# Output mixers of a two-block network: inputs and weight splits taken into the latent attention, first two tiles interleaved

## What is computed

```
for l in range(2):
    h = rms_norm(x, norm_w[l]) * (1 + scale) + shift
    proj = h @ w_in[l]                           # split by columns
    r_o = rms_norm(retention(rope(rq), rope(rk), rv))
    m_o = mla(mq, mkv, mkr, ...)                 # latent attention, 8 heads
    g_o = rms_norm(gla(gq, gk, gv, gg, w_g2[l], b_g2[l]), gla_norm[l])
    mixed = concat(r_o * silu(rz), m_o * silu(mz), g_o * silu(gz))
    x = x + gate * (mixed @ w_out[l])
return rms_norm(x, final_norm)
```

## Time and profile before

| | us |
|---|---|
| median of 3 runs (4027.2 to 4030.54) | 4028.1 |
| the profiled execution, its own time | 4022.91 |
| its span, first to last instruction | 4021.1 |
| of it: second latent attention (3581.0 to 3804.9) | 223.9 |
| start of the second mixer, to its first projection product (3804.9 to 3867.3) | 62.4 |
| start of the first mixer (3057.4 to 3119.6) | 62.2 |

### The profile page before, as it was taken

The page is one execution under the profiler, slowest core; times in us unless marked ns, Lnnn a source line. Parts: engine busy times, 40 slices in busy tenths (PEclk is TensorE's granted clock), DMA queues, the critical chain, the costliest instruction groups (busy, mean ns, idle before and its releaser), DMA issues. The chain is left out here.

```text
span 4021.1 us, 52306 instructions
## 1 busy us (share of the span) xinstructions
PE 3400.3 (85%) x17620; PEld 2687.7 (67%) x17620; DVE 2374.9 (59%) x3722; ACT 1875.8 (47%) x3128; POOL 308.8 (8%) x374
## 2 busy tenths in 40 slices
PE   8988979599999448786999992699895979989778
PEld 7876658488888324575888882578674757877656
DVE  3226666799988637548999885551234645313276
ACT  3115641378888310115788882331345623224474
POOL 0000001000000110000000002000001300000032
PEclk9999989699999769887999996899997989999879
DMA  6322234499999665436999996442223234322232
GB/s 236 106 69 62 64 99 165 161 399 398 399 398 398 240 242 184 160 129 229 399 398 399 399 398 216 168 157 81 61 49 119 98 134 157 115 59 49 74 130 78
DMA packets 411311, 791.67 MB, mean 197 GB/s; under 512 B 99942, under 2 KB 154758, under 8 KB 408968
## 3 DMA queue, kind: packets, MB, share of 16 engines
q1 hardware_dynamic: 388108, 705.61, 48.6%
q0 software_dynamic: 13824, 50.34, 3.6%
q10 hardware_dynamic: 9216, 33.56, 2.1%
HBM read 653.45 MB, written 135.95 MB: 196 GB/s over the span
## 5 line engine op out<-in xcount | busy, mean ns | idle before, releaser
L312 DVE TENSOR_TENSOR experts_down_lo<-weights_down,experts_down_hi 128x1024 fp32r<-128x1024 f32 x256 | 301.1, 1222 | 56.5 <-ACT experts_down_hi L308 54.2
L312 DVE TENSOR_TENSOR experts_gate_lo<-weights_gate,experts_gate_hi 128x1024 fp32r<-128x1024 f32 x256 | 298.8, 1222 | 52.1 <-ACT experts_gate_hi L308 51.4
L308 ACT CAST experts_gate_hi<-weights_gate 128x1024 fp32r<-128x1024 f32 x256 | 254.2, 1056 | 106.5 <-PEq L126 67.8
L312 DVE TENSOR_TENSOR experts_up_lo<-weights_up,experts_up_hi 128x1024 fp32r<-128x1024 f32 x256 | 296.3, 1221 | 1.2 <-ACT experts_up_hi L308 0.5
L359 PE MATMUL project_acc<-project_wh,project_hh 128*128 128x512 f32 (+2 forms) x768 | 286.1, 373 | 0.0
L360 PE MATMUL project_acc<-project_wl,project_hh 128*128 128x512 f32 (+2 forms) x768 | 282.3, 368 | 0.0
L361 PE MATMUL project_acc<-project_wh,project_hl 128*128 128x512 f32 (+2 forms) x768 | 282.3, 368 | 0.0
L308 ACT CAST experts_down_hi<-weights_down 128x1024 fp32r<-128x1024 f32 x256 | 255.8, 1052 | 24.9 <-DMA weights_down<-in_moe_w_down_dram 24.7
L308 ACT CAST experts_up_hi<-weights_up 128x1024 fp32r<-128x1024 f32 x256 | 253.9, 1056 | 7.8 <-DMA weights_up<-in_moe_w_up_dram 6.2
L2248 ACT COPY project_row<-project_acc 128x512 f32<-128x512 f32 (+2 forms) x96 | 51.8, 540 | 380.0 <-PE project_acc L361 380.0
L359 PE MATMUL experts_yp<-experts_down_hi,experts_hTh 128*128 128x512 f32 x512 | 210.6, 411 | 13.1 <-DVE experts_hTl L312 13.1
(11 more groups left out here) (427 smaller groups left out, 8045.8 us busy)
## 6 DMA issues: line engine op xcount, KB each, us to landing
weights_gate<-in_moe_w_gate_dram SPq DMA_DIRECT2D x256, 512.0 KB, 12.9
weights_up<-in_moe_w_up_dram SPq DMA_DIRECT2D x256, 512.0 KB, 12.2
weights_down<-in_moe_w_down_dram SPq DMA_DIRECT2D x256, 512.0 KB, 11.4
scratch_y<-experts_y ACTq DMA_DIRECT2D x64, 512.0 KB, 6.3
pool_ada<-in_ada_w_dram SPq DMA_DIRECT2D x16, 1536.0 KB, 7.7
project_raw<-in_w_in_dram SPq DMA_DIRECT2D x8, 2048.0 KB, 9.8
scratch_proj<-project_row SPq DMA_DIRECT2D x64, 256.0 KB, 2.0
qkv_raw<-in_attn_w_qkv_dram SPq DMA_DIRECT2D x48, 256.0 KB, 3.4
```

What stands on the lines that cost most here:

```text
L308: return act.copy(hi, src)
L312: return dve.tensor_tensor(lo, src, hi.bitcast(F32), ALU.subtract)
```

## The change

A new holder, `MixAhead`, spans the attention and the mixer of a layer. It owns `w` (now with 2 stages of raw rows), `g2`, `bg`, `gn`, `row` and `vv`, and their semaphores; it is a `Phase` of its own, with its own exit. The attention gets it as `prefetch`. SyncE issues, behind the loads of the first two heads, two rows of the weights, the three small vectors, and row tiles and values 0 and 1; later heads load weight rows 2 to 7. In the third pair of each head ScalarE and VectorE split one row.

The mixer starts without these. SyncE loads the attention's output rows, the output gate (with a semaphore of its own, first waited for ahead of the first residual), the final gain and the residual. The chains of tiles 0 and 1 are written interleaved; tile 1 puts its gate products into the bank of `acc[0]` (`small_bank`), `elast` has two places, and `gla_scores` waits for the parts of the tile before. From i = 1 the loops are the ones of before.

```
@@ phase_attention @@
                 load_q(1)
                 load_v(1)
+                if prefetch:
+                    prefetch.load_first(nc, sp)
...
                         load_q(h + 2)
+                    if prefetch and h + 2 < KC:
+                        prefetch.w.load(sp, h + 2)
...
                         for mp in range(maps):
                             exp(n + 1, 1, mp)
+                    if prefetch and i == 2:
+                        prefetch.w.split_hi(act, n // PAIRS)
...
                     if what == "q" and h < HEADS:
                         copy_q(part, h)
+                    if prefetch and n % PAIRS == 2:
+                        prefetch.w.split_lo(dve, n // PAIRS)
@@ new class MixAhead(Phase) @@
+        self.w = SplitRows(self, self.w_out, stages=2)
...
+    def load_first(self, nc, sp):
+        for k in range(2):
+            self.w.load(sp, k)
+        sp.dma_start(self.g2[:, :], self.w_g2).then_inc(self.small_in, 16)
...
+        sp.dma_start(self.gn[:, :], self.gla_norm.partition_broadcast(P)).then_inc(self.small_in, 16)
+        for i in range(2):
+            self.load_row(sp, i)
+            self.load_vv(sp, i)
@@ phase_mix_out @@
-    SMALL = 80 if final else 64
+    SMALL = 48
...
+        def small_bank(i):
+
+            return acc[0][:, :].rearrange("p (a b) -> p a b", a=4) if i == 1 else sc
...
                 pe.wait_ge(q_past, i + 1)
-                Tr(sc[:, 2, :], kwT[:, :], K["ident"]).then_inc(kwt_ready, 1)
+                if i > 0:
+                    pe.wait_ge(ag_ready, i)
+                Tr(small_bank(i)[:, 2, :], kwT[:, :], K["ident"]).then_inc(kwt_ready, 1)
...
                 open_tile(1)
+                gate_and_retention(1)
                 gla_scores(0)
                 updates(0)
-                gate_and_retention(1)
-                for i in range(T):
+                gla_scores(1)
+                outputs(0)
+                open_tile(2)
+                updates(1)
+                gate_and_retention(2)
+                mixed_transposes(0)
+                for i in range(1, T):
@@ ScalarE @@
                 copies(0)
                 softplus(0)
-                w.split_hi(act, 0)
+                copies(1)
                 exponents(0)
...
+                softplus(1)
+                exponents(1)
                 silus(0)
                 silus(1)
...
+                take_outputs(0)
+                copies(2)
+                silus(2)
@@ VectorE @@
                 gate_sums(0)
-                w.split_lo(dve, 0)
+                gate_in(1)
+                retention_scores(1)
                 gla_operands(0)
-                w.split_lo(dve, 1)
+                gate_sums(1)
                 gla_parts(0)
-                w.split_lo(dve, 2)
                 states(0)
-                for i in range(T + 2):
+                gla_operands(1)
+                gla_parts(1)
+                mean_squares(0)
+                gated(0)
+                states(1)
+                normalized(0)
+                for i in range(1, T + 2):
@@ body @@
+                with MixAhead(nc, f"ahead{l}", proj, A["gla_w_g2_2"][l], A["gla_b_g2_2"][r, :], A["gla_norm_2"][r, :],
+                              A["w_out_2"][l]) as ahead:
+                    mla_attention(nc, K, f"mla{l}", mq, mk, mkv, mla_o, totals, ahead)
```

More of the change, by code:

```diff
@@ L2363, in _, with mla_attention @@
                         finish_mla(j)
-def mla_attention(nc, K, name, mq, mk, mkv, out, totals):
+def mla_attention(nc, K, name, mq, mk, mkv, out, totals, ahead):
     def tiles(ap, base, step, width):
@@ L2370, in mla_attention, with __init__, __enter__, load_row @@
     phase_attention(nc, K, name, tiles(mq, 0, MQ, MQ), tiles(mk, 0, MQ, MQ), tiles(mkv, NOPE, NOPE + MV, MV),
-                    tiles(out, 0, MV, MV), 1, MQ, MV, K["chunked"], MQ ** -0.5, totals)
-def phase_mix_out(nc, K, name, proj, mla_o, x, w_g2, b_g2, gla_norm, w_out, mod, final_norm, out):
+                    tiles(out, 0, MV, MV), 1, MQ, MV, K["chunked"], MQ ** -0.5, totals, prefetch=ahead)
+class MixAhead(Phase):
+    SEGS = (("rq", "rk"), ("rz", "rz"), ("mz", "gk"), ("gg", "gz"))
+    ROW = sum(COLS[b][1] - COLS[a][0] for a, b in SEGS)
+    def __init__(self, nc, name, proj, w_g2, b_g2, gla_norm, w_out):
+        super().__init__(nc, name)
+        self.proj, self.w_g2, self.b_g2, self.gla_norm, self.w_out = proj, w_g2, b_g2, gla_norm, w_out
+    def __enter__(self):
+        super().__enter__()
+        self.w = SplitRows(self, self.w_out, stages=2)
+        self.g2, self.bg, self.gn = self.sb("g2", [GRANK, P]), self.sb("bg", [P, 1]), self.sb("gn", [P, GDV])
+        self.row = self.sb("row", [P, 2, self.ROW])
+        self.vv = self.sb("vv", [P, 2, 2, 256])
+        self.small_in = self.sem("small_in")
+        self.row_in, self.vv_in = ([self.sem(f"{n}{b}") for b in range(2)] for n in ("row_in", "vv_in"))
+        return self
+    def load_row(self, sp, i):
+        at = 0
+        for a, b in self.SEGS:
+            c0, c1 = COLS[a][0], COLS[b][1]
+            sp.dma_start(self.row[:, i % 2, at:at + c1 - c0], self.proj[i * P:(i + 1) * P, c0:c1]).then_inc(self.row_in[i % 2], 16)
+            at += c1 - c0
+    def load_vv(self, sp, i):
+        for n, c in enumerate(("rv", "gv")):
+            sp.dma_start(self.vv[:, i % 2, n, :], self.proj[i * P:(i + 1) * P, COLS[c][0]:COLS[c][1]]).then_inc(self.vv_in[i % 2], 16)
+    def load_first(self, nc, sp):
+        for k in range(2):
+            self.w.load(sp, k)
+        sp.dma_start(self.g2[:, :], self.w_g2).then_inc(self.small_in, 16)
+        with nc.allow_non_contiguous_dma(reason="one bias per partition"):
+            sp.dma_start(self.bg[:, :], self.b_g2.rearrange("o (p a) -> p (o a)", a=1)).then_inc(self.small_in, 16)
+        sp.dma_start(self.gn[:, :], self.gla_norm.partition_broadcast(P)).then_inc(self.small_in, 16)
+        for i in range(2):
+            self.load_row(sp, i)
+            self.load_vv(sp, i)
@@ L2382, in phase_mix_out @@
+def phase_mix_out(nc, K, name, ahead, mla_o, x, mod, final_norm, out):
     T = TILES
     final = final_norm is not None
-    SEGS = (("rq", "rk"), ("rz", "rz"), ("mz", "gk"), ("gg", "gz"))
+    SEGS = ahead.SEGS
     at, col_at = 0, {}
@@ L2788, in _ @@
                         softplus(i + 1)
-                    if i == 0:
-                        for k in range(6, KC):
-                            w.split_hi(act, k)
                     if has(i):
@@ L2940, in _ @@
                         final_scale(i - 2)
-                    if i == 0:
-                        for k in range(4, 6):
-                            w.split_lo(dve, k)
                     if has(i):
```

117 lines of the change are left out of this document (43 added, 74 removed).

## The result

The changed kernel takes 4046.1 us (median of 20 runs, 4009.0 to 4075.6) against 4027.9 of the kernel before (20 runs, 4020.5 to 4033.4): ratio 1.0047, 95% interval 1.0032 to 1.0062. It is **slower by 18 us**, where 10 us less was forecast, and outside the range given; the slowest of the twenty, over 1.5% above the fastest, is left out of the ratio. The scatter is a result too: 67 us between its runs, 13 us before. The clock granted to TensorE, averaged over an execution, goes with it: 0.925 in the run of 4009.0 us, 0.915 in the profiled one, 0.909 in the one of 4075.6.

What follows compares the result with a forecast made beforehand. TensorE was taken to bound the attention and steady mixer, with time to win in the two starts. Starts -40.8, stalls +25.6, clock +4, exit +1 gave -10.2 us: 4017.9 from 4028.1, range 3994 to 4036.

Steps and rivals of the forecast that it cites:

- The starts: Stage start to first projection product in each mixer: falls from 62.4 to 42.0 us, -20.4 per mixer, -40.8 for two.
- operands of tile 1 to the end of its scores: 3.5 us: Step in the mixer's start, after tile 0's states at 22.0: takes 3.5 us, done at 25.5.
- the bound of 46: Slow bound of the mixer's start: about 46 us (-16) if GpSimd's scaling slows VectorE's operands and tile 1's scores come late.
- The stalls: Attention: VectorE's subtraction delays maxima and scaled outputs, TensorE waits 1.6 us per head, 8 heads, 2 layers: +25.6 us.
- The rival that hid the splits by busy shares: Attention: splits cost nothing, as ScalarE and VectorE idle half of each head; -40, 3988 us; chance 0.13.
- The clock: Attention: stalls may drop TensorE's granted clock; three falls assumed, +4 us, bounds 0 to 24.
- Three falls: Attention: of 16 stalls, three taken to drop TensorE's clock, as they are shorter than the 1.79 us known to drop it.
- the work of about three microseconds at half rate, 1.5 us: Attention: the price of one fall of TensorE's clock, 1.5 us.
- The stated bound of 24 us for 16 stalls: Attention: upper bound on the cost of clock falls, 0 to 24 us for 16 stalls.
- The rival with a fall at every head: Attention: TensorE's clock falls at each of 16 stalls, 24 us in place of 4; +10, 4038 us; chance 0.12.
- The second exit: Stage boundary: the new buffer holder adds a semaphore clearing and a barrier per layer, 0.5 us each, +1.
- the signs named ahead: Starts of 42 us; attention: subtraction idle until the cast, TensorE idle about 1.8 us 16 times, 12 to 14 us longer per layer.

Runs made afterwards that it cites:

- experiment 7: Experiment 1 with GpSimd's scaling of tile 0's silus held until VectorE finished tile 1's operands and the copy behind them; 3986.8 us, ratio 0.9895.
- experiment 2: The changed kernel with 12 dummy transposes on TensorE ahead of its wait for the scaled outputs in each head's last pair; 4014.7 us, ratio 0.9964.
- experiment 1: The changed kernel with VectorE's subtraction of a weight row one pair later in each head, behind that pair's scaled outputs; 3990.4 us, ratio 0.9911.

## Why the prediction was wrong

**The starts: -40.8 forecast, -36.0 measured.** The chain went as worked out up to tile 0's states: 22.0 us forecast, and tile 1's operands, right behind them, start at 3866.26, 21.9 us in. The step that failed is the next one, "operands of tile 1 to the end of its scores: 3.5 us". It took 6.9 (3866.26 to 3873.17), as VectorE's operands ran beside GpSimd (experiment 7); the first projection product came at 45.0 and 43.6, near the bound of 46 that was given for exactly this. The forecast took the undisturbed value although it had GpSimd next to the operands in its own text. It also never asked what the start would be without the interleaving: the gain was put down to the edit as a whole. Loads and splits alone give 24 us per mixer, and the interleaving takes 6 of them away.

**The stalls: +25.6 forecast, 24.6 measured** (236.4 - 224.1 = 12.3 per layer where the clock holds; 24.3 in experiment 2). The waits themselves are 11.1 of the 12.3 (seven of 1.46 and one of 0.84); the rest stands in the last head, where the clock falls some 7 us earlier than in experiment 1. Mechanism and place were right, and the size nearly. The rival that hid the splits by busy shares is refuted by the 1.46 us in the changed kernel's rows; experiment 1 shows that they can be hidden, but one pair later.

**The clock: +4 forecast, about +30 measured.** (31.5 by experiment 2; in the profiled execution 13.7 + 42.9 - 24.6 = 32.0.) This is the step that made the sign wrong, in both of its factors, the number of falls and the price of one. "Three falls" took the shortest idle time known to have dropped the clock, 1.79 us, as an edge, and stalls below it as nearly safe. Here 1.46, 0.92 and 0.65 us are enough, each at some places and not at others. And "the work of about three microseconds at half rate, 1.5 us" took one length for every fall. The earlier trace rows show only a microsecond of the one behind it, which lasts 3.4 us in the trace; behind the new idle times the clock stayed at half for 3.4 to 20.5 us, costing 1.6 to 8.8. The stated bound of 24 us for 16 stalls was too low for the same reason. The rival with a fall at every head was nearest, with its argument that stalls recurring at one distance might all be hit or none: that is what the two layers show, seven of seven and none of seven. Why it is the one here and the other there stays open. Its price of 16 x 1.5 is not what happens, as the falls differ fivefold in cost.

**The second exit: +1 forecast.** From the first mixer's first projection product to the second attention it is 459.0 us, where it was 461.4. No cost shows there; what made the 2.4 us was not looked into.

**Sum by the measured terms:** -36.0 + 24.6 + 31.5 - 2.4 = +17.7, where the medians differ by 18.2. It mixes differences of medians with stages of one profiled pair, in which untouched code ahead of the attention adds 3.9, so the close match is in part luck. With the clock up, as in experiment 2, the kernel stands at 4014.7, near the 4017.9 forecast: the clock is the one term that the forecast needed.

Of the signs named ahead, the subtraction's idle time, TensorE's before the output products (1.46 us 14 times and 0.84 twice, for 1.8 us 16 times) and the starts' length were all found, and the 12 to 14 us of a layer in the first layer only; the one named as making it wrong, a granted clock visibly below 1.00 in the attention, is what is seen.

## What to carry to other kernels

Work for an engine that is idle half of the time was free here only in the slot where its inputs were already there: look at what stands behind it in order, and put it behind the last thing that somebody waits for, not ahead of it. Where TensorE bounds a stage as here, count each new idle time twice, once for its length and once for the clock, and price the second from the whole low stretch; if a wait can't be removed, filling it with dummy products gave back all of the second part here. A scatter that grows with a change (13 us to 67) was a sign of the clock here: compare the granted clock of the fastest and the slowest run. When an edit has two halves, run the simpler half alone: the interleaving cost 6 us per mixer, beneath a gain of 24.

## What was not expected of the hardware

The same length of idle time does different things in different stages. In the steady part of the second mixer, before the change, TensorE waits 1.05 us once per tile:

```profile
3968.16 0.50 PE L2668 MATMUL mixout_acc<-mixout_w_hi,mixout_mh 128*128 128x512 f32 x1 [1.05 <-DVE mixout_ml L312]
```

five times, besides once 1.20 and once 1.84 us, and the clock is 0.99 over that stage. In the attention, 0.92 us drops it behind 6 of 14 waits. Nor does the length decide within one stage: 1.46 us dropped it behind all seven waits of one layer and behind none of the other, in one execution. What TensorE did before and how dense its products are may matter; the runs here don't settle it.

The stretch at half clock varies as much, 3.4, 6.8, 10.2 or 20.5 us, and TensorE can be busy throughout (20.06 of 20.50). Each attention also begins with such a stretch in every kernel, the one before among them, though there TensorE is idle for part of it (second attention, before):

```profile
3581.00:3598.00 17.00, 10.20 (x30) 0.51 0.55 124
```

Beside GpSimd, VectorE's operations on two operands in SBUF (the on-chip memory) take two to five times as long (1.34 us for 0.28, 1.75 for 0.68) in the rows of experiment 7. The forecast had this only as the bound of 46 us for the start.
